# A two-block layer with 16 experts: weight loads of three, three and two slots, and the first expert's tokens picked by counted ranks

## What is computed

```python
def _expert_choice_ffn(h, norm_g, w_router, w_gate, w_up, w_down):
    u = _rmsnorm(h, norm_g)
    aff = jax.nn.softmax(jnp.einsum('bnd,de->bne', u, w_router).astype(jnp.float32), axis=-1)
    cap = EC_CAPACITY * n_ // N_EXPERTS                 # 2 * 272 // 16 = 34
    g, idx = lax.top_k(jnp.swapaxes(aff, 1, 2), cap)
    xs = jax.vmap(lambda ub, ib: ub[ib])(u, idx)
    hid = (jax.nn.silu(jnp.einsum('becd,edf->becf', xs, w_gate))
           * jnp.einsum('becd,edf->becf', xs, w_up))
    y = jnp.einsum('becf,efd->becd', hid, w_down) * g[..., None].astype(h.dtype)
    return jnp.zeros_like(h).at[jnp.arange(b_)[:, None, None], idx].add(y)
```

## Time and profile before

| what | us |
|---|---|
| median of 3 executions | 2229.68 |
| the three | 2220.01, 2231.13, 2229.68 |
| the profiled execution, its own time | 2224.37 |
| its span | 2222.6 |
| TensorE busy | 2093.5 (94%) |
| VectorE busy | 776.8 (35%) |
| ScalarE busy | 627.7 (28%) |

### The profile page before, as it was taken

One profiled execution on the slowest core, in us unless ns is written; L12 is line 12 of the kernel. 1 busy time (PEld: TensorE's weight loads), 2 busy tenths in 40 slices (PEclk: granted clock), 3 DMA queues, 4 the chain that ended last, 5 costly groups with the idle time before them and its releaser, 6 DMA issues.

```text
span 2222.6 us, 27210 instructions
## 1 busy us (share of the span) xinstructions
PE 2093.5 (94%) x12048; PEld 1308.0 (59%) x12048; DVE 776.8 (35%) x1125; ACT 627.7 (28%) x988; POOL 44.8 (2%) x74
## 2 busy tenths in 40 slices
PE   9999999899898998989899899889999999999999
PEld 9987443333333443334343333327988998988997
DVE  8984211011010111111011011016666565876553
ACT  6664100000000000000000000005555444965442
POOL 3201000000000000000000000000000000000000
PEclk9999999999999999999999999999999999999999
DMA  7529999999999999999999999997444656554653
GB/s 235 173 86 377 421 429 430 428 430 428 430 430 425 430 429 430 428 431 428 429 430 428 431 429 429 430 427 259 152 152 152 214 197 196 174 172 150 197 190 114
DMA packets 146095, 725.21 MB, mean 326 GB/s; under 512 B 8630, under 2 KB 106346, under 8 KB 119482
## 3 DMA queue, kind: packets, MB, share of 16 engines
q1 hardware_dynamic: 144792, 721.47, 81.0%
q0 software_dynamic: 640, 1.37, 0.2%
q10 hardware_dynamic: 546, 0.63, 0.1%
HBM read 722.38 MB, written 1.07 MB: 326 GB/s over the span
## 4 chain that ended last, share of the span: by engine, by line
PE 69%; DMA 27%; DVE 2%; ACT 1%; SPq 1%; issue 0%; DVEq 0%; ACTq 0%
PE bank L1379 24%; PE bank L1254 18%; DMA weight_ring<-in_w_up_dram 9%; DMA weight_ring<-in_w_gate_dram 9%; DMA weight_ring<-in_w_down_dram 7%; PE bank L1334 6%; PE bank L1221 5%; PE bank L872 4%; PE bank L1410 3%; PE bank L1185 1%; PE bank L1071 1%; PE bank L1309 1%; PE bank L1596 1%; PE bank L1726 1%; PE bank L1619 1%; PE bank L1358 1%
## 5 line engine op out<-in xcount | busy, mean ns | idle before, releaser
L1254 PE MATMUL bank<-weight_ring,arena 128*64 128x506 f32 x3024 | 634.9, 566 | 62.9 <-DMA weight_ring<-in_w_up_dram 40.7
L1254 PEld LDWEIGHTS bank<-weight_ring,arena 128*64 128x64 f32 x3024 | 221.9, 135 | 460.4 <-issue 374.4
L1334 PE MATMUL bank<-weight_ring,arena 128*64 128x512 f32 x1408 | 318.5, 602 | 47.0 <-DMA weight_ring<-in_w_down_dram 47.0
L2871 DVE TENSOR_TENSOR weights_ring<-weight_ring,weights_ring 128x2048 fp32r<-128x2048 f32 x110 | 249.7, 2289 | 126.3 <-ACT weights_ring L2158 126.1
L1379 PE MATMUL bank<-input_high,weights_ring 128*128 128x256 f32 x1920 | 245.7, 280 | 0.8 <-issue 0.8
L1334 PEld LDWEIGHTS bank<-weight_ring,arena 128*64 128x64 f32 x1408 | 98.1, 138 | 247.6 <-issue 180.7
L1379 PEld LDWEIGHTS bank<-input_high,weights_ring 128*128 128x128 f32 x1920 | 232.0, 188 | 3.2 <-issue 2.7
L2158 ACT ACTIVATE weights_ring<-weight_ring 128x2048 fp32r<-128x2048 f32 x109 | 205.8, 1908 | 60.7 <-DMA weight_ring<-in_w_ffn_down_dram 41.1
L2828 DVE TENSOR_TENSOR arena<-arena,bank 128x512 f32<-128x512 f32 x48 | 33.0, 688 | 500.2 <-PE bank L1221 500.2
L2054 ACT ACTIVATE arena<-bank 128x506 f32<-128x506 f32 (+1 forms) x48 | 23.5, 562 | 399.0 <-PE bank L1254 399.0
L1379 PE MATMUL bank<-input_low,weights_ring 128*128 128x256 f32 x960 | 130.9, 278 | 0.0
(11 more groups left out here) (427 smaller groups left out, 2078.9 us busy)
## 6 DMA issues: line engine op xcount, KB each, us to landing
weight_ring<-in_w_down_dram SPq DMA_DIRECT2D x62, 2816.0 KB, 21.8
weight_ring<-in_w_up_dram SPq DMA_DIRECT2D x61, 2816.0 KB, 19.5
weight_ring<-in_w_gate_dram SPq DMA_DIRECT2D x60, 2816.0 KB, 18.9
weight_ring<-in_w_ffn_gu_dram SPq DMA_DIRECT2D x44, 1024.0 KB, 5.1
weight_ring<-in_w_ffn_down_dram SPq DMA_DIRECT2D x22, 1024.0 KB, 4.9
weight_ring<-in_w_in_dram SPq DMA_DIRECT2D x16, 1024.0 KB, 6.3
arena<-in_w_xkv_dram SPq DMA_DIRECT2D x8, 2048.0 KB, 20.2
weight_ring<-in_ab_w_in_dram SPq DMA_DIRECT2D x12, 1024.0 KB, 8.0
```

Source lines behind the costliest of these rows:

```text
L1254: last = pe.matmul(bank[first_bank + c][MPAD * half:MPAD * half + MPAD, 0:(hi - lo) * HF], xs3[:, s, :], w[:, lo:hi, HF * half:HF * half + ...
L1334: last = pe.matmul(bank[6][MPAD * half:MPAD * half + MPAD, :], hidT[:, at:at + MPAD], W[:, j * D + 512 * half:j * D + 512 * half + 512], s ...
L2871: dve.tensor_tensor(low_slot(k), raw_slot(k), high_slot(k), ALU.subtract).then_inc(S("weights_low"), 1)
```

## The change

There are four edits.

1. **Loads.** From expert 1 on a matrix comes in three loads, of slots 0 to 2, 3 to 5 and 6 to 7 (`group_load`), each behind the count of its last slot. Expert 0's loads and the last expert's down matrix keep their pairs. 15 gate, 15 up and 14 down matrices have three loads in place of four.
2. **Two up slots earlier.** Slots 6 and 7 of expert 0's up matrix have tiles of their own that the retention frees: the first is loaded when the last retention scores are done, the second when its last values are. Slot 5 stays behind `y_ready`, slot 4 behind `norm_sum`. `memtok`, `mem_squares` and `mT` move in the arena to make room.
3. **Ranks by counting.** Expert 0's tokens don't wait for the five rounds. TensorE spreads expert 0's affinities over all partitions as a row (three transposes); eight `scalar_tensor_tensor` instructions compare that row with each token's own affinity and add up how many tokens are larger (or equal and earlier, with the new table `before`); the sum is the token's rank, and three `tensor_scalar` compare it with 0 to 33. The five rounds for all experts follow, and their results are turned back inside expert 0's gate product (`choice_rows`, after slot 4). The products of `ones` are gone.
4. **Order on ScalarE and VectorE.** The squares of the memory tokens come after expert 0's gathered rows, and the two norms of the memory tokens after expert 0's hidden values.

```diff
+        GROUPS = [(0, 3), (3, 6), (6, 8)]
+        GROUP_AT = {first: n for n, (first, _) in enumerate(GROUPS)}
-        ahead = z((ESLOTS - AHEAD_SLOT) * DFF, 0)
+        ahead = [z(DFF, at) for at in (0, 2816, 7680, 13280)]
...
+            def group_load(name, e, n):
+                first, end = GROUPS[n]
+                sp.dma_start(W[:, first * DFF:end * DFF], rows_of(name, e)[:, first * DFF:end * DFF]).then_inc(landed(n), 16)
...
             sp.wait_ge(S("proj_ready"), 2 * last_a_use(0))
             first_gate_load(0)
+            sp.wait_ge(S("hm_ready"), H)
+            sp.wait_ge(S("r_scores"), H)
+            ahead_load(AHEAD_SLOT + 2)
+            sp.wait_ge(S("ret_ready"), H)
+            sp.dma_start(before, t["before"]).then_inc(S("tokens_landed"), 16)
+            ahead_load(AHEAD_SLOT + 3)
             sp.wait_ge(S("y_ready"), 2 * H)
             sp.dma_start(tiles(memtok, 2), mem).then_inc(S("tokens_landed"), 16)
-            ahead_load(AHEAD_SLOT + 1, ESLOTS)
+            ahead_load(AHEAD_SLOT + 1)
...
             for e in range(1, EXP):
-                for g in range(PAIRS):
-
-                    sp.wait_ge(S("down_used"), 8 * e - 8 + 2 * g + 2)
-                    pair_load("w_gate", e, g)
+                for n, (_, end) in enumerate(GROUPS):
+                    sp.wait_ge(S("down_used"), 8 * e - 8 + end)
+                    group_load("w_gate", e, n)
                 rest_of_expert(e)
...
                     for m in range(TT):
+                        last = pe.transpose(bank[7][:, P * m:P * m + ROWS[m]], a3[0:ROWS[m], m, 0:1].to_broadcast([ROWS[m], P]),
+                                            ident[0:ROWS[m], 0:ROWS[m]])
+                    last.then_inc(S("affT_ready"), 1)
...
+                    if e == 0 and use == 1 and s == 4:
+                        choice_rows()
...
-            for n in range(4):
-                pe.matmul(bank[7][:, 0:P], ones[:], ones[:], start=True, stop=True)
             gather_first()
             for b in range(2):
                 pe.wait_ge(S("rows_taken"), b + 1)
+                if b == 1:
+                    pe.wait_ge(S("choice_steps"), 1)
...
+            row, used = bank[7][:, 0:T], 0
+            for j in range(TT):
+                r, lo = ROWS[j], P * j
+                parts = [(2, ALU.is_equal, lo, lo + r, before[0:r, 0:r]), (1, ALU.is_gt, lo, T, ones[0:r, 0:1].to_broadcast([r, T - lo]))]
+                if j:
+                    parts.append((0, ALU.is_ge, 0, lo, ones[0:r, 0:1].to_broadcast([r, lo])))
+                for part, op, lo_col, hi_col, mask in parts:
+                    n = hi_col - lo_col
+                    last = dve.scalar_tensor_tensor(out=compared[0:r, used:used + n], in0=row[0:r, lo_col:hi_col],
+                                                    scalar=a3[0:r, j, 0:1], in1=mask, op0=op, op1=ALU.mult,
+                                                    accum_out=tallies[0:r, 3 * j + part:3 * j + part + 1])
+                    used += n
+            after(last)
+            after(dve.tensor_reduce(rank, tiles(tallies, TT), AX.X, ALU.add))
+            dve.wait_ge(S("pool_steps"), 1)
+            dve.wait_ge(S("iota_landed"), 16)
+            for j in range(TT):
+                dve.tensor_scalar(ste3[:, j, 0:CAP], iota_row[:, 0:CAP], rank[:, j:j + 1], None, ALU.is_equal).then_inc(S("ste_ready"), 1)
```

More of the change, by code:

```diff
@@ L620, in rest_of_expert, with ahead_load @@
                     pair_load("w_down", e, g)
-            def ahead_load(first, end):
-                sp.dma_start(ahead[:, (first - AHEAD_SLOT) * DFF:(end - AHEAD_SLOT) * DFF], rows_of("w_up", 0)[:, first * DFF:end * DFF])\
+            def ahead_load(slot):
+                sp.dma_start(ahead[slot - AHEAD_SLOT], rows_of("w_up", 0)[:, slot * DFF:(slot + 1) * DFF])\
                   .then_inc(S("apart_landed"), 16)
@@ L1318, in _ @@
                 pairs = 0
+                down_starts = [0, 2, 4, 6] if e in (0, EXP - 1) else [first for first, _ in GROUPS]
                 for j in range(FT):
@@ L1321, in _ @@
                         pe.wait_ge(S("hidT_taken"), 3 * e + j // 4 + 1)
-                    while pairs <= DOWN_SLOT[j] // 2:
-                        pair_landed(pe, e, pairs, 3)
+                    while pairs < len(down_starts) and down_starts[pairs] <= DOWN_SLOT[j]:
+                        if e == EXP - 1 and pairs == PAIRS - 2:
+                            pe.wait_ge(landed(2 * pairs), 16 * (A_USES[2 * pairs] + 2))
+                        else:
+                            pair_landed(pe, e, pairs, 3)
                         pairs += 1
@@ L2043, in _ @@
                                ACT.Copy).then_inc(S("xs_taken"), 1)
+            act.wait_ge(S("utok_taken"), 10)
+            m_T, m_sq = tiles(mT, KT), tiles(mem_squares, KT)
+            for q in range(4):
+                act.activation(m_sq[:, 2 * q:2 * q + 2, :], m_T[:, 2 * q:2 * q + 2, :], ACT.Square).then_inc(S("norm_squares"), 1)
             def take_slots(e):
@@ L2782, in _ @@
             last.then_inc(S("aff_ready"), 1)
+            ste3, c3 = tiles(STe, TT), tiles(counts, TT)
             dve.wait_ge(S("affT_ready"), 1)
+            dve.wait_ge(S("tokens_landed"), MEM_TOKENS)
+            row, used = bank[7][:, 0:T], 0
[14 more added lines that the diff above has]
+            dve.wait_ge(S("iota_landed"), 16)
+            for j in range(TT):
+                dve.tensor_scalar(ste3[:, j, 0:CAP], iota_row[:, 0:CAP], rank[:, j:j + 1], None, ALU.is_equal).then_inc(S("ste_ready"), 1)
+            dve.wait_ge(S("affT_ready"), 2)
             src = bank[5][0:EXP, 0:T]
```

94 lines of the change are left out of this document (53 added, 41 removed).

## The result

The changed kernel is slower: 2235.32 us, the median of 22 executions, against 2228.14 for 22 of the kernel before, a ratio of 1.0030 [1.0022, 1.0039], so +6.7 us (the two medians themselves are 7.2 us apart). The forecast was 2224 with a range to 2235. The profiled execution took 2237.78 us, its span is 2236.0 us.

A forecast was written before the change was run, and what follows sets the result against it. It took TensorE's chain as the bound until about 258 us, then the DMA rate to the experts' end. Terms 0.4 - 4 + 0.5 = -3.1 us gave 2221.3 on the profiled execution, 2226.6 on the median; it predicted 2224, range 2214 to 2235.

The forecast's parts named there:

- Holes in the file: Expert transfers: loads of three are issued later, worst at each down product's first group with 3.6 us left; counted 0.5 us.
- +0.4: Expert 1's first load: issued at 258.0, 0.4 us later; waiting for a third slot costs 2.6, TensorE comes 2.2 earlier.
- Long waits mean that TensorE is ahead: Expert stage: the argument against holes deciding, that TensorE's longer waits for landings show it ahead of the transfers.
- the rival: First load issued in each down product: half clock after waits opens holes, +18 us in full, +7 for half; chance 0.12.
- The rate: Expert loads: 44 matrices with one load less save packet costs, 3.0 to 4.7 us, taken as 4.
- The first rival: Expert loads: only the head start counts, the rate gain is an artefact; about +1 us, 2228; chance 0.17.
- The ranks: Expert 0's front end: counted ranks start the gather and the gate product 2.8 us earlier, the latter at 204.8.
- the third rival: Expert 0's front end: the ranks come no earlier, by costly compares or late counts; +2.8 us, so 2227; chance 0.1.
- The early up slots: Expert 0's up matrix: two slots loaded while the DMA engines are idle; a gain of 0 from this edit alone.
- The fourth rival: Expert loads: each load costs more than its packets, 0.2 us a load; the whole is -8 us, 2219; chance 0.11.

The follow-up runs named there:

- e3: The changed kernel with 14 products of ones, whose result nobody reads, ahead of ten gate products to hold the clock; ratio to the kernel before 1.0004.
- e9: The changed kernel with only gate matrices in loads of three, three and two slots, up and down matrices in pairs; ratio to the kernel before 1.0003.
- e1: The changed kernel with all its loads as pairs again, early up slots, counted ranks and engine order kept; ratio to the kernel before 0.9985.
- e2: The changed kernel with loads of two, three and three slots in place of three, three and two; ratio to the kernel before 1.0009.
- e6: The changed kernel with gate matrices in pairs, up and down matrices in loads of three, three and two slots; ratio to the kernel before 0.9992.
- e10: The kernel of e6 measured once more, on another chip; ratio to the kernel before 0.9988.
- e11: The kernel of e1 measured once more, on another chip; ratio to the kernel before 0.9987.
- e12: The kernel of e6 with 14 products of ones ahead of ten gate products, as in e3; ratio to the kernel before 0.9983.
- e7: The changed kernel with pairs for experts 5 to 10, and 14 products of ones ahead of the gates of experts 2 to 5 and 12 to 15; ratio 1.0003.
- e8: The kernel of e1 without the early up slots: slots 6 and 7 load behind `y_ready`; ratio to the kernel before 1.0003.
- e4: The changed kernel with issues as late, but each group of three cut in loads of two and one, 5 loads a matrix; ratio to before 1.0013.
- the mix: The kernel of e6 and e10: gate matrices in pairs, up and down in loads of three, three and two; ratios to before 0.9992 and 0.9988.

## Why the prediction was wrong

- **The step that failed is "Holes in the file".** The term was set at +0.5 us and is +11.2 between the two traces, so the sum of +0.4 - 4 + 0.5 = -3.1 becomes +0.7 - 4.1 + 11.2 = +7.8, against 8.9 in these two executions and 6.7 by the ratio. The mechanism had been written down, half clock after waits of 4.7 us once a matrix (they are 4.46 to 4.73 at ten gate products), and as a rival it had a chance of 0.12, with +7 as its half size. It was the right one in its cause, though the place that it named, the first load issued in each down product, is the smaller of two.
- **Why the term was mis-sized.** It was worked out at one place, the gate loads behind the down product, called the worst, with 3.6 us to spare. That place has 3.9 us of holes, and 3.6 of them stand where `kv_block` products lie between the rows of the down product; the working had put such blocks in the gate product alone. There the lateness needs no half clock: from 655 to 684 us the granted clock is 1.00 in the changed kernel, and the second gate load, at 683.0, still opens a hole of 1.0 us (0.8 at the same place in e3). The larger part, 7.4 us, is at the up loads behind the gate product, where the long wait stands directly ahead of the product whose reads release the loads. There the count was never made: 7.3 us in hand at full clock, 4.8 to 5.6 at half. e3 shows this part by holding the clock, e9 by taking the up matrix's threes away.
- **"Long waits mean that TensorE is ahead"** was the argument against the rival, and it is where I went wrong in weighing. TensorE waits because what it waits for lands in larger pieces; what it has in hand for the transfers is less, not more: 13.0 us with pairs, 7.3 with threes at full clock.
- **How much in hand is enough.** I took 2.5 us for an issue to flow, and 2 more for the rest. In the rows above 4.5 us in hand ends in a hole of 1.1 us, 5.6 in one of under 0.1; 7.3 and 6.2 (e3's first and second up load) in none. The count can be made for every load of the fourteen traces, by the bytes that are issued and not yet moved, at 430 GB/s. It gives about 2 us less than the count by landings (2.5, 3.6, 5.5 and 4.3 us for these four), for about that much of the transfers behind a landing has moved when the landing is told. Of the loads of three slots 68 of 78 that were issued with under 2.5 us of bytes left stand at a hole, 29 of 63 between 2.5 and 3.5, 1 of 42 between 3.5 and 4, and none of 420 above.
- **The rate** was right: 4.1 us by 431.7 against 430.3, forecast 3.0 to 4.7, taken 4. The packet's own cost, 11 ns, is inside the 8.4 to 13 of the two lines. The first rival, that the rate was an artefact, falls.
- **The ranks** were right: 2.5 us earlier at the gate product (2.8 forecast), so the third rival falls. (POOL's clearing, which was put before 199, released the last three compares at 199.2, still ahead of TensorE.) Over the executions with ranks, early slots and a first load of two slots at expert 1 (e1, e2, e6, e10, e11, e12) the first load is issued at 255.0 on average, 2.6 us ahead of the one execution of before, 257.6 (2.2 worked out), though single ones lie between 253.9 and 256.6. With a first load of three (changed, e3, e7, e9) the mean is 258.0, the forecast's number: the third slot takes it all.
- **The early up slots**: nothing seen at the stage's marks, as forecast, within 2 us; e8's median leaves it open.
- **The fourth rival**, more than a packet's cost per load, falls with e4: 5, 4 and 3 loads a matrix are equal steps of 1.4 GB/s.
- Still open: how much of the 3.9 us at the gate loads is clock (2.6 are left with the clock held at ten of fifteen gate products), why the mix keeps 3 us of holes at its up loads, and what of the file neither rate nor holes explain: 1 us in the changed kernel, 3 in e3.

## What to carry to other kernels

When transfers are the bound and a ring is refilled as it is read, work out for every place where a load is released how many us of transfers are in hand at that moment, at full clock and at half, and not only for the place that looks worst. In these traces a load of three slots issued with 4 us of bytes or more still to move left no hole. Larger loads take from that twice, since the reader starts later and releases later; here three slots in place of two brought 4 us of rate and cost 11 us of holes. Look also for other work between the reads, such as the `kv_block` products here, for it delays the release as half clock does. A DMA share of 1.00 hides it: compare the rate of the best slices with the mean, and look at the clock.

## What was unexpected of the hardware

- TensorE at 91% busy still drops to half clock: in waits of about 4.5 us for a landing, or within 1 us behind them, the granted clock fell to the lower of its two levels (1.2 of 2.4 GHz) and the next twelve matmuls took 4.3 to 5.0 us in place of 2.6. Shorter waits differ between executions: behind one of 2.19 us near 505 us it stayed high in e1 and fell in e11, the same kernel.
- A load issued with little in hand starts slowly: around such issues packets of 33.8 KB took up to 3.3 us in place of 1.25. Why is not settled.
- The second block, which the change doesn't touch, has two speeds. Windows of 50 us at nearly the same place in it (232 and 233 us behind the last scatter), before and then after:

```profile
1745.00:1795.00 50.00, 50.00 (x443) 50.00 (x443) 30.76 (x24) 22.99 (x19) 0.00 (x0) 1.00 0.61 198
```

```profile
1755.00:1805.00 50.00, 50.00 (x427) 50.00 (x426) 28.75 (x22) 23.29 (x19) 0.00 (x0) 1.00 0.58 189
```

TensorE does 443 or 427 instructions, 113 or 117 ns each, at a granted clock of 1.00 in both. The stretch from the last scatter to the end takes 709.1 to 709.8 us in eight of the fourteen profiled executions and 712.7 to 714.1 in six; the kernel of e6 and e10 has one of each (709.7 and 713.8). There is more than one such place: e4 also does 427 instructions there, but has the short end (709.7), for it is 4 us faster than all others in the last 230 us. What chooses between them was not found. It is as large as the effects measured here, which is why the stage's own marks were compared.
